# A hybrid two-layer block: the MoE's wide and narrow experts streamed and multiplied in alternating turns, gathered by one set of products

## The reference, cut to what matters

```
def moe_swiglu(h, router, w1, w3, w2):          # 8 experts, 2 per token, D=1024, F=3584
    logits = t @ router;  top_v, top_i = top_k(logits, 2);  top_p = softmax(top_v)
    gate = sum(one_hot(top_i) * top_p)
    for e in range(8):
        y = y + gate[:, e:e+1] * ((silu(t @ w1[e]) * (t @ w3[e])) @ w2[e])
```

## Time and profile before

| | us |
|---|---|
| median of 3 runs | 1685.98 (1683.12 to 1688.79) |
| the profiled execution's own time | 1682.87 |
| its span, first to last instruction | 1681.1 |
| TensorE matmul busy | 1617.6 (96%) |
| VectorE, ScalarE busy | 612.4 (36%), 447.4 (27%) |
| DMA over the span | 472.75 MB, mean 281 GB/s |

### The profile page before, as it was taken

The page is one execution under the profiler, slowest core; times in us unless marked ns, Lnnn a source line. Parts: engine busy times, 40 slices in busy tenths (PEclk is TensorE's granted clock), DMA queues, the critical chain, the costliest instruction groups (busy, mean ns, idle before and its releaser), DMA issues.

```text
span 1681.1 us, 34749 instructions
## 1 busy us (share of the span) xinstructions
PE 1617.6 (96%) x15676; PEld 1091.0 (65%) x15676; DVE 612.4 (36%) x1036; ACT 447.4 (27%) x693; POOL 32.3 (2%) x27
## 2 busy tenths in 40 slices
PE   6999999999999999999999999999999999899995
PEld 6977767799988977777866534565345643356431
DVE  3667685645544677775510010101111010010101
ACT  3554533544533555533300000000100010000101
POOL 0000030000000000030000000000000000000000
PEclk9989999999999989999999999999999999999998
DMA  6423413345653423413989999999999999999993
GB/s 253 176 101 126 150 52 126 140 178 186 228 204 145 176 101 127 150 53 125 409 320 382 363 423 427 426 426 424 427 428 425 425 425 428 427 425 425 426 428 164
DMA packets 41108, 472.75 MB, mean 281 GB/s; under 512 B 4544, under 2 KB 4544, under 8 KB 5632
## 3 DMA queue, kind: packets, MB, share of 16 engines
q1 hardware_dynamic: 40592, 468.86, 69.2%
q0 software_dynamic: 368, 1.65, 0.2%
HBM read 469.44 MB, written 1.05 MB: 280 GB/s over the span
## 4 chain that ended last, share of the span: by engine, by line
PE 82%; DMA 9%; DVE 5%; ACT 2%; issue 1%; SPq 0%; DVEq 0%; ACTq 0%
PE bank L608 69%; DMA pairs_high<-stream 6%; DMA pairs_low<-stream 2%; DVE ring_a_r L1708 1%; PE bank L1221 1%; DVE arena L1708 1%; PE bank L1285 1%; PE bank L690 1%; PE bank L984 1%; DVE arena L1714 1%; PE bank L895 1%; ACT high_a L1378 1%; DMA smalls<-small 1%; PE bank L804 1%; PE bank L976 1%
## 5 line engine op out<-in xcount | busy, mean ns | idle before, releaser
L608 PE MATMUL bank<-pairs_high,hsel 128*32 128x256 f32 (+1 forms) x4320 | 334.6, 408 | 4.2 <-DMA pairs_high<-stream 4.2
L608 PEld LDWEIGHTS bank<-pairs_high,hsel 128*32 128x32 f32 (+1 forms) x4320 | 161.9, 113 | 161.2 <-issue 83.3
L1708 DVE TENSOR_TENSOR ring_a_r<-ring_a,high_a 128x2048 fp32r<-128x2048 f32 x82 | 188.0, 2296 | 125.0 <-ACT high_a L1378 124.9
L1708 DVE TENSOR_TENSOR arena<-arena,bank 128x256 f32<-128x256 f32 (+2 forms) x122 | 44.5, 392 | 465.7 <-ACT arena L1631 452.9
L1378 ACT ACTIVATE high_a<-ring_a 128x2048 fp32r<-128x2048 f32 x82 | 157.1, 1916 | 135.8 <-PE bank L608 117.0
L608 PE MATMUL bank<-pairs_high,actT 128*32 128x256 f32 (+1 forms) x2048 | 165.0, 413 | 7.3 <-DMA pairs_high<-stream 7.3
L608 PE MATMUL bank<-hT_h,ring_a_r 128*128 128x256 f32 (+1 forms) x592 | 167.4, 283 | 0.0
L608 PE MATMUL bank<-high_a,hT_h 128*128 128x512 f32 (+1 forms) x416 | 165.0, 397 | 0.8 <-issue 0.8
L608 PE MATMUL bank<-pairs_low,hsel 128*32 128x256 f32 (+1 forms) x1952 | 161.9, 415 | 0.2 <-DMA pairs_low<-stream 0.2
L608 PE MATMUL bank<-ring_a_r,hT_h 128*128 128x512 f32 (+1 forms) x416 | 159.7, 384 | 0.0
L608 PE MATMUL bank<-high_a,hT_l 128*128 128x512 f32 (+1 forms) x416 | 159.6, 384 | 0.0
(11 more groups left out here) (324 smaller groups left out, 1790.3 us busy)
## 6 DMA issues: line engine op xcount, KB each, us to landing
pairs_high<-stream SPq DMA_DIRECT2D x113, 2048.0 KB, 27.5
pairs_low<-stream SPq DMA_DIRECT2D x55, 2048.0 KB, 27.4
ring_a<-stream SPq DMA_DIRECT2D x107, 1024.0 KB, 4.8
consts<-const SPq DMA_DIRECT2D x1, 1079.0 KB, 7.1
resid<-x SPq DMA_DIRECT2D x1, 1024.0 KB, 5.0
y<-xn SPq DMA_DIRECT2D x2, 512.0 KB, 2.7
smalls<-small SPq DMA_DIRECT2D x1, 824.5 KB, 10.7
smalls<-small POOLq DMA_DIRECT2D x1, 824.5 KB, 7.1
```

Of the source, the lines that this page charges most:

```text
L608: ins = mm(o, lhsT, rhs, start=start, stop=stop)
L1708: return v.tensor_tensor(o, i0, i1, op)
```

## The change

The eight places become four pairs of places (`TURNS`): a wide and a narrow place at a time, in alternating turns of one up group (4 pieces) or one down group (2 pieces). In the pairs 1 to 3 the order is wide up 0, narrow up 0, wide up 1, ... narrow up 6, wide down 0, narrow down 0, ... In pair 0 the wide place (expert 0) goes ahead by four up groups, 16 pieces, because the second place's expert is not known before the routing; then narrow and wide alternate, and the last four turns are narrow downs alone.

- The ring becomes 16 pieces (8 loads) instead of 18, and none of its slots waits for `router_logits`. `hsel`, `hsel_n`, `actT`, `actT_n` lie elsewhere.
- `gather_pair`: 16 products of 160 columns (96 + 64) take the place of 16 of 96 and 16 of 64; the first `up` of each pair of places waits until both `hsel` and `hsel_n` are written (6 VectorE instructions instead of 2 for a place).
- `scatter_pair`: for each token tile and half, three products of the wide place and three of the narrow one accumulate in one bank, then one add; 4 adds for a pair of places instead of 8. The narrow halves no longer follow one another directly.
- The narrow downs accumulate in bank 7. The scatter of a pair of places follows the first two turns of the next, its gather the turn after the last up.
- `keep_busy` reads `iota` in place of `masks`.

```diff
-RING, RING_EXPERT, RING_OVER = 5, 18, 14
+RING, RING_EXPERT, RING_OVER = 5, 16, 14
...
+TURNS = []
+for _p in range(EXPERTS // 2):
+    _lead = 4 if _p == 0 else 0
+    _wide = [(UP, True, g) for g in range(EXP_GROUPS)] + [(DOWN, True, g) for g in range(EXP_GROUPS)]
+    _narrow = [(UP, False, g) for g in range(EXP_GROUPS)] + [(DOWN, False, g) for g in range(EXP_GROUPS)]
+    _pair = _wide[:_lead]
+    for _w, _n in zip(_wide[_lead:] + [None] * _lead, _narrow):
+        _pair += [_t for _t in ((_n, _w) if _lead else (_w, _n)) if _t]
+    TURNS.append(_pair)
...
+        def scatter_wide(half, tt, alone):
+            o, cols = pb[4 + half][:, :], slice(half * 512, half * 512 + 512)
+            mm(o, pickT_h[0:HOLD, tsl(tt)], yexp_h[0:HOLD, cols], start=True, stop=False)
+            mm(o, pickT_h[0:HOLD, tsl(tt)], yexp_l[0:HOLD, cols], start=False, stop=False)
+            return mm(o, pickT_l[0:HOLD, tsl(tt)], yexp_h[0:HOLD, cols], start=False, stop=alone)
...
+        def gather_pair(p):
+            pe.wait_ge(sem("main_pick"), p + 1)
+            if p:
+
+                pe.wait_ge(sem("main_act"), p * PAIR_UPS)
+                pe.wait_ge(sem("main_pickT"), p)
+            for k in range(KC):
+                at = k % 3 * (HOLD + P // 2)
+                for tt in range(TT):
+                    ins = mm(pb[k // 3][:, at:at + HOLD + P // 2], xn[:, tt, k * P:k * P + P], picks[:, tt, :], start=tt == 0, stop=tt == 1)
...
+        def experts_pair(p):
...
+                    if u >= 2:
+                        pe.wait_ge(sem("main_act"), u - 1)
+                    up("main_", n0, wide, 2 * (u % 2))
...
+                if p and t < TT:
+                    if t == 0:
+                        yexp_ready(p - 1)
+                    scatter_pair(p - 1, t)
+                if t == last_up + 1 and p + 1 < len(TURNS):
+                    gather_pair(p + 1)
...
+        def yexp_pair(p):
+            yexp_in("main_", p)
+            ve.wait_ge(sem("main_down_n"), p + 1)
+            v.tensor_copy(yexp_n, pb[7][:, :]).then_inc(sem("main_yexp_n"), 1)
+            yexp_low("main_", p)
```

More of the change, by code:

```diff
@@ L175 @@
 OVERS = len(OVER_PLACE)
+UP, DOWN = "up", "down"
+TURNS = []
[7 more added lines that the diff above has]
+    TURNS.append(_pair)
+AHEAD = 16
+TURN_AT, TURN_UP = [], []
+_at = _up = 0
+for _pair in TURNS:
+    TURN_AT.append([])
+    TURN_UP.append([])
+    for _kind, _, _ in _pair:
+        TURN_AT[-1].append(_at)
+        TURN_UP[-1].append(_up)
+        _at += 4 if _kind == UP else 2
+        _up += _kind == UP
+PAIR_UPS = 2 * EXP_GROUPS
 def ring_slot(n):
@@ L1229, in scatter @@
[L1229 to L1245, removed]
-                    ins = mm(pb[4 + half][:, :], lhs[hs, tsl(tt)], rhs[hs, 0:512], start=rhs is not yexp_l and lhs is pickT_h, stop=lhs is pickT_l)
-                    if lhs is pickT_l:
-                        ins.then_inc(sem(tag + "scattered"), 1)
+            here = 4 if wide else KC
@@ L2287, in gate_up @@
             ins.then_inc(sem(tag + "act"), 1)
-        def expert(tag, wide, before, k, s, following):
-            hsel_in(tag, wide, k)
-            if s is not None:
-                yexp_in(tag, s, before)
-            for g in range(1, EXP_GROUPS + 1):
-                gate_up(tag, wide, k, g - 1)
-                if s is not None and g <= TT:
-                    add(tag, s, g - 1)
-                if g == TT:
-                    ve.wait_ge(sem(tag + "pickT_hi"), k + 1)
-                    rows = slice(0, HOLD if wide else P)
-                    tt_(pickT_l[rows, :], pb[7][rows, 0:T], pickT_h[rows, :].bitcast(F32), ALU.subtract).then_inc(sem(tag + "pickT"), 1)
-                if g == 4:
-                    following()
@@ L2314, in _ @@
-        yexp_in("main_", EXPERTS - 1, WIDE[-1])
+        hsel_pair(0)
+        pickT_low(0)
+        for p, pair in enumerate(TURNS):
+            if p:
+                yexp_pair(p - 1)
+            for t, (kind, wide, g) in enumerate(pair):
+                if kind == UP:
+                    ve.wait_ge(sem("main_silu"), TURN_UP[p][t] + 1)
+                    gate_up("main_", wide, TURN_UP[p][t] % 2)
+                if p and t < TT:
+                    add("main_", p - 1, t)
+                if p and t == TT:
+                    pickT_low(p)
+                if t == 8 and p + 1 < len(TURNS):
+                    ve.wait_ge(sem("main_turned_weights"), 2 * p + 2)
+                    choose_pair(p + 1)
+            if p + 1 < len(TURNS):
+                hsel_pair(p + 1)
```

462 lines of the change are left out of this document (279 added, 183 removed).

## The result

The changed kernel takes 1693.05 us in the median of 8 runs (1688.67 to 1697.79); the kernel before, run beside it, 1684.55 us in 8 runs (1677.52 to 1688.79). The ratio is 1.0057, with the interval 1.0037 to 1.0076: **slower by 0.57%, 8.5 us**. That lies inside the range of the prediction (1679 to 1697), but 5 us over its value of 1688.0, and beyond its "no measurable change". It is the place where the first rival stood (1692.5).

What follows compares the result with a forecast made beforehand. Loads, not TensorE, were taken to bind the kernel. Last load 3.7 us earlier, tail 5.2 later, 0.5 for the clock: +2.0 us, median 1685.98 to 1688.0, no measurable change; range 1679 to 1697.

Steps and rivals of the forecast that it cites:

- the first rival: Final scatter runs at half clock after a longer TensorE idle time: 5.5 us more for 24 products, 1692.5 us; chance 0.17.
- The bound: Loads bind from load 33 on: 208.8 us per pair of places, against 201.1 us of TensorE before and 206 after.
- The second rival: TensorE becomes the bound if changes between wide and narrow products cost more than assumed: 1696 us; chance 0.13.
- the third: Each load takes 4.88 us instead of 4.97, 14 us over 152 loads: 1674 us; chance 0.12.
- Start: Ahead of the first up: choices +1.0, wider gather +0.9, transposes and writes +0.4 us; first up at 848.3, +2.3 us.
- Loading: First up to last landing: lead, then narrow and wide alternating at the loads' pace; last load at 1657.5, 3.7 us earlier.
- The 16th load: In the lead: slot released 43.9 us after the first up at 848.3, landing 8.9 us later, at 901.1.
- 152 loads: Steady state after 901.1: 4.97 us each, ending at 1656.5; taken as 1657.5 for the larger wide share.
- Tail: Behind the last landing: late wide down, wide low part and longer scatter, together +5.2 us.
- The term of the change of shape and the wide low part: Tail before the scatter: late wide down plus switch between wide and narrow products +0.7, wide low part +1.3 us.
- The scatter at full clock: End of the tail: four halves and one add take about 7.9 us where 4.73 were needed, +3.2 us.
- the 0.5 us for the clock: Allowance in the sum for the chance that the clock is low in the tail: 0.5 us.

Runs made afterwards that it cites:

- e4: Changed kernel without three of the eight channel blocks in every wide up, output no longer the reference's; one run, 1686.71 us against 1683.43 of the kernel before.
- e5: Changed kernel with pairs 1 to 3 doing seven wide downs, then seven narrow ones; 1694.67 us, ratio 1.0075 to the kernel before.
- e2: Changed kernel with `keep_busy` reading `masks` again, but for two products; 1691.06 us, ratio 1.0039 to the kernel before.
- e7: e5's order plus wide low part by itself, early wide scatter, 4 constant products, then narrow products in twos; 1685.01 us, ratio 1.0000 to the kernel before.
- e9: e7 without its four products of constants; 1682.63 us, ratio 0.999 to the kernel before.
- e10: Changed kernel with a ring of 14 pieces (seven loads) instead of 16; 1698.94 us, ratio 1.010 to the kernel before.
- e12: Changed kernel, unchanged, profiled a second time; 1692.86 us in the profiled execution.
- e1: Changed kernel with 15 products of constants between the last down and the last scatter; 1690.1 us, ratio 1.0034 to the kernel before.
- e3: Changed kernel with the scatter's six wide products first, then the narrow ones of both halves in turns; 1688.49 us, ratio 1.003 to the kernel before.
- e6: Changed kernel with the first wide place chosen and gathered alone, the narrow gather after the second up; 1696.82 us, ratio 1.0066 to the kernel before.
- e8: Edits of e7 and e6 together; 1685.09 us, ratio 1.0013 to the kernel before.

## Why the prediction was right or wrong

**The bound: right.** The loads bind before and after. e4 shows it by taking work from TensorE, e5 by taking changes of shape from it. The second rival (TensorE becomes the bound) falls with e5, the third (a pace of 4.88) with the 4.984 of the changed kernel, and e4 doesn't reach it either.

**Start: the term was right, its surroundings were not.** Predicted +2.3 us, measured +2.0 where the clock stood. But two traces out of two of the changed kernel have a half clock in the routing, 2.9 us more, and no term or rival of the prediction held that. Among the twelve traces with the changed kernel or a variant it is there in eight (after, e2, e4, e5, e7, e9, e10, e12) and not in four (e1, e3, e6, e8); in the two of the kernel before it is absent. It costs 2.9 us in six of the eight, 3.7 in e2 and 5.3 in e4. Most traces start their router near one of three times. Near 824 the starts at 824.02 and 824.32 lost the clock, those at 824.40, 824.45 and 824.64 kept it. Near 828.7 those at 828.52, 828.56 and 828.69 lost it, 828.71 and 828.84 kept it, but these two are the kernel before. Near 832.8 the start at 832.69 lost it, 832.84 kept it. Two starts stand alone, 826.17 and 829.76, and lost it. In each group the later ones keep the clock, and in the first and the last all are the changed kernel or a variant. That points to the moment at which the routing starts rather than to the change, but it is argued only: no run moves that moment on purpose. Whether the changed kernel meets the fall more often stays open. An estimate from the stages: without it the sum is 2.0 - 3.4 + 9.6 = 8.2 us, and by the repeats 2.0 - 3.0 + 9.8 = 8.8, so the 8.5 us between the medians don't need it.

**Loading: right mechanism, a gain half as large.** Predicted from first up to last landing 809.2 us (1657.5 - 848.3), 6 less than before; measured 811.69, 3.4 less, and 3.0 less between the repeats. Two terms are short. The 16th load was to land 52.8 us after the first up; it did so after 54.1, since its slot came free at 44.4 instead of 43.9 and the transfer took 9.7 us instead of 8.9. In the repeat e12 that transfer took 8.2 us and the landing came after 52.6, so this part differs between executions. And 152 loads took 4.984 us each, not 4.97, 2.1 us in all, of which I had added 1 for the wide share. That part repeats (4.983 in e12). The kernel before, too, was 2.0 us shorter here in its repeat than in the one trace that I had read. With the late start the last load lands 1.3 us later than before, where the prediction had it 3.7 earlier.

**Tail: the parts right, the clock wrong.** The term of the change of shape and the wide low part was 2.0 us; landing to scatter grew by 1.6 (5.9 to 7.53). The scatter at full clock was to take 7.9 us and takes 8.06 (e1). A change of shape in it costs 0.2 us at full clock (1.79 for a half of six products, less 6 x 0.23, by two), not 0.25. These make 4.9 of the 5.2 us predicted. **The step that failed is the 0.5 us for the clock, that is the 0.17 that I gave to the first rival: the scatter was to run at full clock, and it ran at half, for 4.7 us.** The prediction's own sign of it, products 0.43 us apart, is there. The rows to see it were there: an idle stretch of 2.18 us and then a fall of the clock towards the end of the scatter, and a change that makes the stretch 1.1 us longer and the work behind it 8 us instead of 4.7. The clock fell ahead of or in the scatter in each of the eight traces that have the unfilled gap of 3.3 us (after, e2 to e6, e10, e12). With the gap filled or closed it did not (e1, e7, e8, e9). The rival had 5 us for it, 4.7 is measured.

**The sum.** Against the spans: start +4.9, loading -3.4, tail +9.6, together +11.1 us, where +2.0 was forecast. 2.9 of the 9 us missing are the clock in the routing, 4.2 the clock in the tail beyond the 0.5 allowed for, 2.6 the smaller gain in the loading; the other terms were too high by 0.6 together. Between the medians it is 8.5 us. The forecast's mistake was to weigh as unlikely a fall of the clock for which the trace had the pattern; of the other sizes only the loading was off by more than half a microsecond. That the time lies in the stated range is owed to the slow rivals, over which the range was drawn, and not to the sum.

## What to carry to other kernels

When a kernel is bound by its loads, only two places still count: the work ahead of the first full ring, and the work behind the last landing. A change in between that makes the stream smoother can gain only what the stream lost before. Here it gained 3 us, and lost more than that at the two ends. Before you lengthen a tail, look at the granted clock row behind each idle gap of TensorE: put independent products into the gap (e9), rather than constants, which have to be sized exactly (e1, e8), and which take twice as long and hold up the work behind them when the clock falls all the same (the routing).

## What was not expected of the hardware

- The clock fell while PE was shown as busy. Within 16 float32 products of 128 x 8 (32 instructions) it went from 1.00 to 0.50 at about 831.1, though 403 to 446 GB/s of loads ran beside it; the five filler products behind them then took 4.61 us instead of 2.40. It came back at 837.9, after 6.8 us; in e2 it took 10.2 us and in e4 13.7.
- In the tail the clock did not come back under dense work. From about 1670.8 to 1682 PE ran product after product of 512 columns and the granted clock stayed 0.50 for 11 us; in e12 for 12.7 us, from the first product to the last (1668.20 to 1680.88).
- A change between 96-row and 64-row products delays two starts, its own and the next. At full clock both are 0.34 us instead of 0.23 (1673.94, 1674.27 and 1674.61 in e1), at half clock 0.55 and 0.60 instead of 0.43 (1671.90, 1672.45 and 1673.05). That is 0.2 and 0.29 us for a change, so it grows by less than the factor of 2 between the clocks.
- A last load of 2 MB, issued at 1627.44, lands 35.0 us later at a full ring, and 9.7 us later at 895.14 when the queue was nearly empty. Its time to landing says how deep the queue is, not how fast.
